# Filler work of an attention stage in smaller pieces, and an expert combination merged with the normalisation that follows it

## The chip, the cores and the metric

The program runs on one core of one Trainium2 chip and is launched once. The metric is the device time of that launch in microseconds (us). The profile is of one execution of the same program.

## The reference, cut to what matters

Two transformer blocks work on 512 tokens of width 1024, in float32. The parts that the change touches:

```python
# first block
mod = silu(c) @ ada_w + ada_b           # six rows of 1024: sh1, sc1, g1, sh2, sc2, g2
h = rms_norm(x, ln1_g) * (1.0 + sc1) + sh1
x = x + g1 * hybrid_mixer(h, w_in, w_out, ...)      # eight NSA heads, eight MoBA heads
h = rms_norm(x, ln2_g) * (1.0 + sc2) + sh2
x = x + g2 * sparse_moe(h, ...)         # per token: sum over 4 experts of gate * y[expert row]
...
# second block
h = rmsnorm(x, norm1_g)
z = h @ w_in                            # then a convolution branch, an attention branch, PEER
```

## The kernel before, in words

The tokens lie as four tiles of 128 rows on the partitions (`env.x`, named x_res in the trace). The program is a row of stages. Each stage is a block in which the five engines run their own lists of instructions and meet only by semaphores; a stage ends in a barrier of all engines (line 173), and nothing of the next stage is issued before it. There is no scheduler: the order on an engine is the order in which the code is written.

**Weights.** `Pieces` brings weights in pieces of 1 MB into four places of a ring (`load`, issued by SP, line 210). A piece for TensorE is split into two parts, so that three products give float32 accuracy: ScalarE rounds the whole piece (`round`, line 232, 128x2048) and VectorE subtracts (`split`, line 241). A piece for the modulation stays raw: `modulate` (lines 313 to 322) multiplies each of its four 512-column slices by an entry of silu(c) and adds it to a row of `mod` (line 320), four passes that depend on each other.

**The attention of the first block** (`attention`, stage att1) goes through 12 heads of 8 steps g: heads 0 to 7 are NSA heads (g = 0 to 63), heads 8 to 11 are pairs of MoBA heads. In a step ScalarE takes the exponential of the scores (line 861), TensorE transposes it (line 782) and starts the scores of step g + 2 (lines 774, 775), VectorE moves the transposed tile out of PSUM (line 889), takes the maximum of the next scores (line 883) and, in steps 1 to 4 of a head, finishes the head before it (lines 899 to 924); in step 4 it also prepares the compressed scores (lines 941 to 944), which ScalarE exponentiates (line 869). Before heads 3, 4, 7 and later more than one operand has to be transposed and moved (lines 765, 853). Two hooks put filler work of later stages between: `act_between(g)` on ScalarE behind the exponential, `dve_between(g)` on VectorE behind the maximum. Before the change VectorE runs four modulation passes in a row at g = 4, 8, 12 and 16, and a whole split at g = 34, 38, 42 and 46; ScalarE rounds a whole piece at g = 33, 37, 41 and 45.

**Experts, combination, normalisation.** `expert_blocks` writes each expert's rows to DRAM (`y_rows`). The stage `combine` (line 1709) gathers 16 tiles of 128 rows into all eight places of the ring with indirect DMAs of GpSimd (line 1723), and VectorE sums four of them per token tile with their gates, multiplies by g2 and adds to x (lines 1730 to 1734). Since the gathered rows fill the ring, the second mixer's first weight pieces can't be loaded until the stage is over. The stage `norm_split` (line 1739, named norm) then loads the gain and four pieces (SP), takes the squares of all four tiles on ScalarE (line 1763) and one square root (line 1765), scales the rows on VectorE (line 1780), transposes them on TensorE (line 1796), rounds and subtracts the transposed tiles (lines 1768, 1783), and last rounds and splits the four pieces (lines 232, 241). Then a barrier, and the stage conv begins with the product of the first piece.

Of the kernel before, what the change touches and what calls it, by code (L numbers as in the profile page):

```python
# [5 lines left out]
F32 = mybir.dt.float32  # L6
# [4 lines left out]
ALU = mybir.AluOpType  # L11
# [3 lines left out]
P = 128  # L15
# [166 lines left out]
class Pieces:  # L182
# [60 lines left out]

    def take(self, pe):
# [67 lines left out]
def modulate(env, pieces, dve, step, mod, c_act, n, first=0, halves=(0, 1)):  # L312

    own = mod[:, ada_tile(LATER[n])]
    for half in halves:
        w = pieces.take_raw(dve)
        if half:
            dve.wait_ge(pieces.summed, 2 * n + 1)
        for k in range(4):
            ins = env.nc.vector.scalar_tensor_tensor(own, w[:, k, :], c_act[:, 4 * half + k:4 * half + k + 1], own, ALU.mult, ALU.add)  # L320
            if k < 3:
                ins.then_inc(step, 1)
                dve.wait_ge(step, (2 * (n - first) + half) * 3 + k + 1)
        ins.then_inc(pieces.summed, 1)
# [624 lines left out]
def nsa_and_moba(env, z, kct, vc, gs, y_dram, pieces, mod, c_act, step):  # L949
# [759 lines left out]
def combine(env, gate, dest, y_dram, g_row):  # L1709

    nc = env.nc
    ctx, sb, ps, sem = stage(nc, "comb")
    with ctx:
        acc = sb("acc", [P, D])
        got = [sem(f"got{t}") for t in range(NT)]
        chain_s = sem("chain")
        block = ctx.enter_context(nc.Block())
        row = lambda n: env.ring[:, n // 2, (n % 2) * D:(n % 2 + 1) * D]

        @block.gpsimd  # L1720
        def _(pool):
            for n in range(NT * TOP_K):
                nc.gpsimd.indirect_dma_start(row(n), None, y_dram, bass.IndirectOffsetOnAxis(dest[:, n:n + 1], 0)).then_inc(got[n // TOP_K], 16)

        @block.vector
        def _(dve):
            chain = Chain(dve, chain_s)
            for t in range(NT):
                dve.wait_ge(got[t], 16 * TOP_K)
# [9 lines left out]
def norm_split(env, ht, h, pieces, gain, first_loads):  # L1739
# [3 lines left out]
    with ctx:  # L1743
# [16 lines left out]
        def _(act):  # L1760
# [8 lines left out]
            for i in range(RAW):  # L1769
                pieces.round(act)  # L1770
# [801 lines left out]
```

## Time and profile before

| what | value |
|---|---|
| median of 3 runs | 3841.49 us (3839.79 to 3841.69) |
| the profiled execution | 3840.8 us |
| its span, first to last instruction | 3838.6 us |
| mean granted TensorE clock | 0.934 of full |
| TensorE busy | 88% of the span |
| VectorE busy | 76% |
| ScalarE busy | 36% |

The busy shares are averages over some fifteen stages with different limits, so they say little about one of them. The clock is given as a share of 2.4 GHz: 0.50 is 1.2 GHz. The attention of the first block lies at 257 to 474 us of the span; the combination, the normalisation and the barriers around them at 1776 to 1844 us.

### The profile page before, as it was taken

How to read it: one execution, taken by the hardware profiler on the slowest of the kernel's cores; microseconds unless marked ns; L12 is line 12 of the kernel's file. 1: busy time of each engine (PE TensorE's matmuls, PEld its weight loads, DVE VectorE, ACT ScalarE, POOL GpSimd, SP SyncE). 2: the span in 40 equal slices, each digit the busy share in tenths (PEclk: the TensorE clock that was granted, in tenths of full speed). 3: DMA queues.
4: the chain of work that ended last, by engine and by line, in shares of the span. 5: the costliest groups of instructions: out<-in, count | busy, mean ns of one | idle time of the engine just before them, and what ended most of it. 6: DMA issues, size and time to landing. Idle time of an engine off the chain costs nothing. (4 is left out here: it accounts for less than half of the span.)

```text
span 3838.6 us, 39707 instructions
## 1 busy us (share of the span) xinstructions
PE 3383.1 (88%) x13912; PEld 2336.3 (61%) x13912; DVE 2909.8 (76%) x4717; ACT 1386.3 (36%) x1678; POOL 720.4 (19%) x720
## 2 busy tenths in 40 slices
PE   7979969999999999993889999878888888888876
PEld 4757757777777777772768687644344443443432
DVE  4566668999999999995788254378888888888885
ACT  2223436777777777772213343111111111111110
POOL 0000001000000000001000010034444444444442
PEclk9957989999999999996899989989999999999999
DMA  5343038999999999994323302299999999999997
GB/s 198 99 168 115 10 126 307 381 367 374 373 366 378 370 369 378 366 371 162 98 77 110 99 1 99 80 377 417 421 415 407 421 413 414 411 420 416 406 421 326
DMA packets 253621, 1106.23 MB, mean 288 GB/s; under 512 B 21233, under 2 KB 30577, under 8 KB 187601
## 3 DMA queue, kind: packets, MB, share of 16 engines
q1 hardware_dynamic: 166130, 521.50, 37.5%
q0 software_dynamic: 80640, 562.07, 35.7%
q10 hardware_dynamic: 6720, 20.97, 1.4%
q8 instruction: 75, 1.23, 0.1%
q14 instruction: 56, 0.46, 0.0%
HBM read 1071.44 MB, written 33.03 MB: 288 GB/s over the span
## 5 line engine op out<-in xcount | busy, mean ns | idle before, releaser
L2298 PE MATMUL peer_acc<-peer_rows,peer_diag 128*128 128x512 f32 x2048 | 983.7, 629 | 218.0 <-DVE peer_diag L2450 217.2
L1634 DVE TENSOR_TENSOR moe_w_lo<-ring,moe_w_hi 128x2048 fp32r<-128x2048 f32 x384 | 861.7, 2286 | 49.4 <-ACT moe_w_hi L1550 49.4
L2298 PEld LDWEIGHTS peer_acc<-peer_rows,peer_diag 128*128 128x128 f32 x2048 | 390.9, 200 | 747.1 <-issue 413.9
L2233 POOL DMA_INDIRECT peer_rows<-in_peer_uv,peer_ids x512 | 578.6, 1130 | 930.4 <-PE peer_acc L2298 682.2
L1550 ACT ACTIVATE moe_w_hi<-ring 128x2048 fp32r<-128x2048 f32 x384 | 713.8, 1913 | 106.4 <-DMA ring<-in_exp_w 68.3
L2445 DVE CUSTOM_DVE_ANT_0 peer_rows<-peer_rows,peer_h 128x1024 f32<-128x1024 f32 x512 | 618.8, 1223 | 158.4 <-DMA peer_rows<-in_peer_uv,peer_ids 149.5
L2357 ACT ACTIVATE peer_gelu<-peer_dot 128x2 f32<-128x2 f32 x256 | 52.0, 203 | 1130.6 <-DVE peer_dot L2445 1130.5
L1413 POOL COPY moe_col<-slots 128x1 uint32 (+1 forms) x32 | 53.0, 1658 | 1068.9 <-PE moe_tp L1442 973.1
L2450 DVE TENSOR_SCALAR peer_diag<-consts_sb,peer_gelu,peer_gates 128x128 f32<-128x128 f32 x512 | 161.5, 389 | 68.3 <-ACT peer_gelu L2357 67.1
L241 DVE TENSOR_TENSOR mix_lo<-ring,mix_hi 128x2048 fp32r<-128x2048 f32 (+1 forms) x56 | 125.6, 2257 | 76.1 <-ACT mix_hi L232 75.4
L1459 PE MATMUL moe_yp<-moe_w_hi,moe_hidt_hi 128*128 128x512 f32 x512 | 168.2, 409 | 2.1 <-DVE moe_hidt_lo L1629 2.1
L1459 PE MATMUL moe_yp<-moe_w_lo,moe_hidt_hi 128*128 128x512 f32 x512 | 163.0, 400 | 0.0
L1972 DVE SCALAR_TENSOR_TENSOR conv_rows<-glu,conv_taps,conv_rows 128x512 f32<-128x512 f32 x240 | 161.2, 757 | 0.5
L1459 PE MATMUL moe_yp<-moe_w_hi,moe_hidt_lo 128*128 128x512 f32 x512 | 161.4, 396 | 0.0
L2261 PEld LDWEIGHTS peer_qps<-peer_ht,ring 128*128 128x128 f32 x1024 | 125.9, 195 | 35.0 <-issue 35.0
L889 DVE COPY spare<-att_pt 128x128 f32<-128x128 f32 (+3 forms) x160 | 78.6, 491 | 87.6 <-PE att_pt L782 84.1
L232 ACT ACTIVATE mix_hi<-ring 128x2048 fp32r<-128x2048 f32 (+1 forms) x56 | 104.9, 1886 | 102.4 <-DMA ring<-in_w_in 45.4
L262 PE MATMUL conv_acc<-mix_hi,ht_hi 128*128 128x512 f32 x320 | 128.3, 401 | 11.8 <-DVE glu L1960 11.8
L774 PE MATMUL att_sc<-spare 66*128 66x128 f32 (+3 forms) x320 | 132.0, 499 | 1.5 <-ACT spare L853 1.5
L2261 PE MATMUL peer_qps<-peer_ht,ring 128*128 128x128 f32 x1024 | 126.6, 278 | 5.4 <-DMA ring<-in_peer_wq 4.7
L263 PE MATMUL conv_acc<-mix_lo,ht_hi 128*128 128x512 f32 x320 | 127.1, 397 | 0.0
L264 PE MATMUL conv_acc<-mix_hi,ht_lo 128*128 128x512 f32 x320 | 127.1, 397 | 0.0
(447 smaller groups left out, 5822.5 us busy)
## 6 DMA issues: line engine op xcount, KB each, us to landing
ring<-in_exp_w SPq DMA_DIRECT2D x384, 1024.0 KB, 7.1
ring<-in_w_in SPq DMA_DIRECT2D x38, 1024.0 KB, 5.2
ring<-in_ada_w SPq DMA_DIRECT2D x16, 1024.0 KB, 7.6
y_rows<-moe_y ACTq DMA_DIRECT2D x32, 512.0 KB, 6.9
ring<-in_ada_w SPq DMA_DIRECT2D x4, 2048.0 KB, 17.9
ring<-in_w_out SPq DMA_DIRECT2D x8, 1024.0 KB, 5.0
ring<-in_peer_wq SPq DMA_DIRECT2D x4, 2048.0 KB, 18.5
peer_rows<-in_peer_uv,peer_ids POOLq DMA_INDIRECT x512, 12.6
```

What stands on the lines that cost most here:

```text
L262: nc.tensor.matmul(out, lhs[0], rhs[0], start=start, stop=False)
L263: nc.tensor.matmul(out, lhs[0], rhs[1], start=False, stop=False)
L774: nc.tensor.matmul(sc[:, g % 2, 0:end], qt[0:AUG, q_place(i, u), t * P:end], kt[0:AUG, k_place(i, u), 0:end], start=True, stop=False)
L1459: last = nc.tensor.matmul(bank[:, q, :], lhs[l][:, k, :], w[:, slot, a * D + q * W:a * D + (q + 1) * W], start=k == 0 and l == 0 and w is ...
L1550: nc.scalar.activation(w_hi[:, slot, :], env.ring[:, slot, :], ACT.Copy).then_inc(hi_done, 1)
L1634: nc.vector.tensor_tensor(w_lo[:, slot, :], env.ring[:, slot, :], w_hi[:, slot, :].bitcast(F32), ALU.subtract).then_inc(lo_done, 1)
L1972: ins = nc.vector.scalar_tensor_tensor(conv[:, n, :], glu[:, n, tap:tap + S], taps[:, n, tap:tap + 1], conv[:, n, :], ALU.mult, ALU.add)
L2233: nc.gpsimd.indirect_dma_start(rows[:, n % SL, :], None, d["peer_uv"], bass.IndirectOffsetOnAxis(ids[:, u % 4, s:s + 1], 0)).then_inc(gath ...
L2261: last = nc.tensor.matmul(qps[:, side, :], wq[head // 2][:, k, at:at + P], ht[:, k, t * P:(t + 1) * P], start=(k == 0), stop=(k == KC - 1))
L2298: last = nc.tensor.matmul(acc[:, t % 2, q, :], diag[:, n % SL], rows[:, n % SL, D + q * W:D + (q + 1) * W], start=first, stop=final)
L2445: nc.vector.tensor_tensor_reduce(left, left, h[:, t, :], 1.0, 0.0, ALU.mult, ALU.add, dot[:, n % SL:n % SL + 1]).then_inc(dotted, 1)
L2450: nc.vector.tensor_scalar(diag[:, n % SL], ident, act_out[:, n % SL:n % SL + 1], gates[:, u % 4, n % K:n % K + 1], ALU.mult, ALU.mult).the ...
```

## The change

In the attention, the same filler work is cut finer and spread. `modulate_op` issues one modulation pass, at each even g from 6 to 36 (16 passes). `round_part` and `split_part` treat a quarter of a piece (128x512): the roundings at each even g from 44 to 74, the splits at each odd g from 55 to 85.

The stages of combination and normalisation become one, `combine_and_norm`. The gathered rows go into the room in which the second mixer later keeps its activations (`got_rows`), so the ring is free and the gain and the four pieces are issued by SP at the stage's beginning, beside GpSimd's gathers. ScalarE scales the first gathered tile of each token tile, and takes square and square root of one tile at a time; VectorE puts the scaling and subtraction of a finished tile between the passes of the next. Two of the four splits move into the stage conv.

```diff
+    def round_part(self, act, q):
+        i, parts, cols = self.of_pe[self.rounds]
+        n = parts * cols // 4
+        cut = slice(q * n, (q + 1) * n)
+        if q == 0:
+            act.wait_ge(self.landed[i % RAW], 16 * (i // RAW + 1))
+            act.wait_ge(self.used, self.rounds - RAW + 1)
+        ins = self.env.nc.scalar.activation(self.hi[:, self.rounds % RAW, cut], self.raw[:, i % RAW, cut], ACT.Copy)
+        if q == 3:
+            ins.then_inc(self.hi_done, 1)
+            self.rounds += 1
...
     def act_between(act, g):
-        if g in (33, 37, 41, 45):
-            pieces.round(act)
+        if 44 <= g < 76 and g % 2 == 0:
+            pieces.round_part(act, (g - 44) // 2 % 4)
 
     def dve_between(dve, g):
-        if g in (4, 8, 12, 16):
-            n, half = divmod(g // 4 - 1, 2)
-            modulate(env, pieces, dve, step, mod, c_act, 6 + n, 6, (half,))
-        if g in (34, 38, 42, 46):
-            pieces.split(dve)
+        if 6 <= g < 38 and g % 2 == 0:
+            at, k = divmod((g - 6) // 2, 4)
+            modulate_op(env, pieces, dve, step, mod, c_act, 6 + at // 2, at % 2, k, at)
+        if 55 <= g < 87 and g % 2:
+            pieces.split_part(dve, (g - 55) // 2 % 4)
...
-def norm_split(env, ht, h, pieces, gain, first_loads):
+def combine_and_norm(env, gate, dest, y_dram, g_row, got_rows, ht, pieces, gain, first_loads):
...
+            def scale_first(t):
+                act.wait_ge(got[t], 16 * TOP_K)
+                nc.scalar.activation(h(t), h(t), ACT.Copy, scale=gate[:, t, 0:1]).then_inc(first, 1)
+
+            act.wait_ge(eps_set, 1)
+            scale_first(0)
+            pieces.round(act)
+            scale_first(1)
+            pieces.round(act)
             for t in range(NT):
-                chain(nc.scalar.activation(junk[:], env.x[:, t, :], ACT.Square, accum_out=ms[:, t:t + 1]))
...
+                act.wait_ge(added, t + 1)
+                chain(nc.scalar.activation(h(t), env.x[:, t, :], ACT.Square, accum_out=ms[:, t:t + 1]))
+                nc.scalar.activation(rstd[:, t:t + 1], ms[:, t:t + 1], ACT.Sqrt, bias=eps[:], scale=1.0 / D).then_inc(root, 1)
+                if t + 2 < NT:
+                    scale_first(t + 2)
+                    pieces.round(act)
+                for n in range(2 * t, 2 * t + 2):
+                    act.wait_ge(turn, n + 1)
+                    nc.scalar.activation(place(ht[0], n), bank(n), ACT.Copy).then_inc(hi_ok, 1)
...
             for t in range(NT):
...
+                own = h(t)
+                dve.wait_ge(got[t], 16 * TOP_K)
+                dve.wait_ge(first, t + 1)
+                for k in range(1, TOP_K):
+                    chain(nc.vector.scalar_tensor_tensor(own, row(t * TOP_K + k), gate[:, t, k:k + 1], own, ALU.mult, ALU.add))
+                    if t == 1 and k == 1:
+                        dve.wait_ge(landed, 16)
+                        normalise(0)
+                    if t > 1 and k == 1:
+                        normalise(t - 1)
+                        rest(t - 2)
+                chain(nc.vector.tensor_tensor(own, own, g_row, ALU.mult))
+                nc.vector.tensor_tensor(env.x[:, t, :], env.x[:, t, :], own, ALU.add).then_inc(added, 1)
+            pieces.split(dve)
+            normalise(NT - 1)
+            rest(NT - 2)
+            pieces.split(dve)
+            rest(NT - 1)
...
             dve.wait_ge(landed, 32)
+            for c in range(2):
+                pieces.split(dve)
             glu_of(0)
```

VectorE, attention, the beginning of head 1 (g = 8 to 12), before. The row on `mod` with x4 is a batch of modulation passes; `att_pt` is the transposed tile, `att_nmax` the maximum:

```order
L889 COPY spare<-att_pt 128x128
L883 TENSOR_REDUCE att_nmax<-att_sc 128x1
L320 SCALAR_TENSOR_TENSOR mod<-ring,c_act,mod 128x512 x4
L889 COPY spare<-att_pt 128x128
L883 TENSOR_REDUCE att_nmax<-att_sc 128x1
L899 RECIPROCAL att_rsum<-att_rsum 128x8
L908 TENSOR_REDUCE att_csum<-att_cs 128x4
L909 TENSOR_TENSOR att_wgt<-gs,att_rsum 128x4
L910 TENSOR_TENSOR att_wgt<-gs,att_rsum 128x4
L911 RECIPROCAL att_csum<-att_csum 128x4
L912 TENSOR_TENSOR att_o<-att_o,att_wgt 128x256
```

The same place now (lines 914 and 920 are the maximum and the move, 347 the modulation):

```order
L920 COPY spare<-att_pt 128x128
L914 TENSOR_REDUCE att_nmax<-att_sc 128x1
L347 SCALAR_TENSOR_TENSOR mod<-ring,c_act,mod 128x512
L920 COPY spare<-att_pt 128x128
L914 TENSOR_REDUCE att_nmax<-att_sc 128x1
...
L943 TENSOR_TENSOR att_o<-att_o,att_wgt 128x256
L920 COPY spare<-att_pt 128x256
L914 TENSOR_REDUCE att_nmax<-att_sc 128x1
L347 SCALAR_TENSOR_TENSOR mod<-ring,c_act,mod 128x512
L945 TENSOR_TENSOR att_csum<-att_csum,consts_sb 128x4
```

One pass now stands behind the maximum of every second step, also of step 2 (shown) and of step 4 of the head.

ScalarE, the beginning of the merged stage now (`mix_hi<-ring` is the rounding of a weight piece, line 1782 the scaling of a gathered tile, line 1791 the squares):

```order
L1782 ACTIVATE got_rows<-got_rows,gate 128x1024
L232 ACTIVATE mix_hi<-ring 128x2048
L1782 ACTIVATE got_rows<-got_rows,gate 128x1024
L232 ACTIVATE mix_hi<-ring 128x2048
L1791 ACTIVATE got_rows,norm_ms<-x_res 128x1024
L1792 ACT_TABLE_LOAD
L1792 ACTIVATE norm_rstd<-norm_ms,norm_eps 128x1
L1782 ACTIVATE got_rows<-got_rows,gate 128x1024
L232 ACTIVATE mix_hi<-ring 128x2048
L1798 ACTIVATE ht_hi<-norm_turned 128x4x128 x2
```

The first two roundings, which before came last in the stage norm, now stand ahead of the first square and square root.

## Rows read from the trace of the kernel before

**Rows 1.** Stretches, heads 0 to 9: us; busy of PE, PEld, DVE, ACT, POOL; clock; DMA.
```profile
256.75:280.17 23.42, 22.12 (x83) 16.64 (x82) 10.48 (x22) 6.11 (x19) 0.53 (x2) 0.50 0.33 117
280.17:302.65 22.48, 20.19 (x110) 16.02 (x109) 16.57 (x39) 6.21 (x20) 0.53 (x2) 0.73 0.28 94
302.65:323.32 20.67, 19.89 (x110) 16.42 (x109) 13.73 (x35) 6.21 (x21) 0.53 (x2) 0.75 0.61 230
323.32:340.51 17.19, 16.48 (x121) 13.96 (x120) 11.21 (x32) 7.06 (x22) 1.79 (x6) 0.96 0.59 243
340.51:362.23 21.72, 19.41 (x108) 15.52 (x106) 15.55 (x33) 9.59 (x22) 0.54 (x2) 0.77 0.00 2
362.23:385.73 23.50, 21.19 (x110) 17.16 (x109) 15.61 (x33) 9.59 (x22) 0.54 (x2) 0.72 0.00 1
385.73:402.17 16.44, 15.62 (x113) 12.85 (x112) 11.14 (x32) 6.09 (x20) 0.54 (x2) 0.98 0.00 0
402.17:418.34 16.17, 15.89 (x123) 13.43 (x121) 11.16 (x32) 7.66 (x24) 2.33 (x8) 1.00 0.01 1
418.34:432.20 13.86, 13.86 (x106) 11.56 (x104) 10.31 (x28) 6.85 (x22) 2.53 (x8) 1.00 0.01 2
432.20:445.42 13.22, 13.22 (x102) 11.04 (x101) 8.45 (x19) 6.88 (x21) 2.11 (x8) 1.00 0.01 2
```
**Rows 2.** Timeline of VectorE in the attention: a filler batch, idle places of head 6.
```profile
292.88 3.10 DVE L320 SCALAR_TENSOR_TENSOR mod<-ring,c_act,mod 128x512 f32<-128x512 f32 x4
...
390.21 0.29 DVE L889 COPY spare<-att_pt 128x128 f32<-128x128 f32 x1 [1.76 <-PE att_pt L782]
...
402.12 0.69 DVE L889 COPY spare<-att_pt 128x512 f32<-128x512 f32 x1 [0.94 <-PE att_pt L782]
```
**Rows 3.** Two stretches of head 2, columns as in the first group.
```profile
312.00:314.00 2.00, 1.67 (x12) 1.47 (x13) 1.82 (x5) 0.88 (x4) 0.00 (x0) 1.00 0.94 294
314.00:316.00 2.00, 2.00 (x11) 1.62 (x10) 1.82 (x5) 0.00 (x0) 0.00 (x0) 0.64 1.01 401
```
**Rows 4.** Timeline of the combination: the first gather, VectorE's first and last tile.
```profile
1775.92 0.94 POOL L1723 DMA_INDIRECT ring<-y_rows,dest  x1 [118.97 <-PEq L1713]
...
1785.91 0.75 DVE L1730 TENSOR_SCALAR comb_acc<-ring,gate 128x1024 f32<-128x1024 f32 x1 [33.87 <-DMA ring<-y_rows,dest]
1786.70 3.93 DVE L1732 SCALAR_TENSOR_TENSOR comb_acc<-ring,gate,comb_acc 128x1024 f32<-128x1024 f32 x3
...
1813.72 1.22 DVE L1734 TENSOR_TENSOR x_res<-x_res,comb_acc 128x1024 f32<-128x1024 f32 x1
```
**Rows 5.** Timeline of the normalisation and the barriers around it, ScalarE and VectorE.
```profile
1816.32 1.06 ACT L1763 ACTIVATE norm_junk<-x_res 128x1024 f32<-128x1024 f32 x1 [49.95 <-PEq L173]
...
1821.02 1.28 ACT L1765 ACT_TABLE_LOAD   x1
1822.32 0.30 ACT L1765 ACTIVATE norm_rstd<-norm_ms,norm_eps 128x4 f32<-128x4 f32 x1
...
1822.64 0.18 DVE L1777 RECIPROCAL norm_rstd<-norm_rstd 128x4 f32<-128x4 f32 x1 [6.22 <-ACT norm_rstd L1765]
1822.86 4.87 DVE L1780 SCALAR_TENSOR_TENSOR h<-x_res,norm_rstd,norm_gain_row 128x1024 f32<-128x1024 f32 x4
1827.65 5.23 DVE L1783 TENSOR_TENSOR ht_lo<-norm_turned,ht_hi 128x512 fp32r<-128x512 f32 x8
1833.76 8.90 DVE L241 TENSOR_TENSOR mix_lo<-ring,mix_hi 128x2048 fp32r<-128x2048 f32 x4 [0.89 <-ACT mix_hi L232]
1843.96 0.06 DVE L1976 MEMSET conv_eps<- 128x1 f32 x1 [1.30 <-PEq L173]
1862.89 0.69 DVE L1960 TENSOR_TENSOR glu<-conv_val,conv_held 128x512 f32<-128x512 f32 x1 [13.07 <-ACT conv_held L1919]
```
**Rows 6.** Stretches of the gathers alone and of the loads of gain and pieces alone.
```profile
1776.00:1802.00 26.00, 0.00 (x0) 0.00 (x0) 15.63 (x14) 0.00 (x0) 16.81 (x16) 0.50 0.86 323
1816.30:1832.00 15.70, 6.39 (x32) 5.78 (x32) 9.21 (x13) 10.81 (x19) 0.00 (x0) 0.56 0.95 300
```
**Rows 7.** The page's group of the roundings (busy, mean ns; idle before).
```profile
L232 ACT ACTIVATE mix_hi<-ring 128x2048 fp32r<-128x2048 f32 (+1 forms) x56 | 104.9, 1886 | 102.4 <-DMA ring<-in_w_in 45.4
```
**Rows 8.** A 512 KB gather of the expert stage: quickest, median, slowest from issue to landing.
```profile
DMA to landing us min/median/max: 4.3/8.0/9.0
```

More of the change, by code:

```diff
@@ L309, in ada_tile, with modulate_op, modulate @@
     return slice(j * W, (j + 1) * W)
-def modulate(env, pieces, dve, step, mod, c_act, n, first=0, halves=(0, 1)):
+def modulate_op(env, pieces, dve, step, mod, c_act, n, half, k, at):
     own = mod[:, ada_tile(LATER[n])]
-    for half in halves:
-        w = pieces.take_raw(dve)
+    if k == 0:
+        pieces.now = pieces.take_raw(dve)
         if half:
             dve.wait_ge(pieces.summed, 2 * n + 1)
-        for k in range(4):
[L320 to L324, printed above, removed]
+    else:
+        dve.wait_ge(step, 3 * at + k)
+    ins = env.nc.vector.scalar_tensor_tensor(own, pieces.now[:, k, :], c_act[:, 4 * half + k:4 * half + k + 1], own, ALU.mult, ALU.add)
+    ins.then_inc(step if k < 3 else pieces.summed, 1)
+def modulate(env, pieces, dve, step, mod, c_act, n, first=0):
+    for half in range(2):
+        for k in range(4):
+            modulate_op(env, pieces, dve, step, mod, c_act, n, half, k, 2 * (n - first) + half)
 def first_norm(env, mod, c_act, ht, z, pieces):
@@ L1706, in _ @@
             dve.sem_inc(tick, 1)
[L1709 to L1729, printed above, removed]
-                chain(nc.vector.tensor_scalar(acc[:], row(t * TOP_K), gate[:, t, 0:1], None, ALU.mult))
-                for k in range(1, TOP_K):
-                    chain(nc.vector.scalar_tensor_tensor(acc[:], row(t * TOP_K + k), gate[:, t, k:k + 1], acc[:], ALU.mult, ALU.add))
-                chain(nc.vector.tensor_tensor(acc[:], acc[:], g_row, ALU.mult))
-                chain(nc.vector.tensor_tensor(env.x[:, t, :], env.x[:, t, :], acc[:], ALU.add))
 C2_GATE, C2_Q, C2_F, C2_GA, C2_GB = D, 2 * D, 5 * D, 5 * D + FOX_HEADS, 6 * D + FOX_HEADS
 PAD = CONV_W - 1
-def norm_split(env, ht, h, pieces, gain, first_loads):
+def combine_and_norm(env, gate, dest, y_dram, g_row, got_rows, ht, pieces, gain, first_loads):
     nc = env.nc
@@ L1743, in norm_split @@
     with ctx:
-        gain_row = sb("gain_row", [P, D]); junk = sb("junk", [P, D])
+        gain_row = sb("gain_row", [P, D])
         ms = sb("ms", [P, NT]); rstd = sb("rstd", [P, NT]); eps = sb("eps", [P, 1])
         turned = ps("turned", [P, 4, W])
-        landed, eps_set, root, ready, turn, hi_ok, lo_ok, act_s, chain_s = (sem(n) for n in (
-            "landed", "eps_set", "root", "ready", "turn", "hi_ok", "lo_ok", "act_chain", "chain"))
+        landed, first, added, root, eps_set, ready, turn, hi_ok, lo_ok, act_s, chain_s = (sem(n) for n in (
+            "landed", "first", "added", "root", "eps_set", "ready", "turn", "hi_ok", "lo_ok", "act_chain", "chain"))
+        got = [sem(f"got{t}") for t in range(NT)]
         block = ctx.enter_context(nc.Block())
+        row = lambda n: got_rows[:, n, :]
+        h = lambda t: got_rows[:, t * TOP_K, :]
         place = lambda a, n: a[:, 4 * (n % 2):4 * (n % 2) + 4, n // 2 * P:(n // 2 + 1) * P]
@@ L1757, in _ @@
             sp.wait_ge(landed, 16)
+        @block.gpsimd
+        def _(pool):
+            for n in range(NT * TOP_K):
+                nc.gpsimd.indirect_dma_start(row(n), None, y_dram, bass.IndirectOffsetOnAxis(dest[:, n:n + 1], 0)).then_inc(got[n // TOP_K], 16)
         @block.scalar
```

47 lines of the change are left out of this document (25 added, 22 removed).

## Prediction

> **What bounds the kernel now.** The page first: TensorE is busy for 88% of the span, VectorE for 76%. That is an average, and the change works in two places only, so I read stretches. In the attention one stretch per head shows what a head costs and at which clock [rows 1]. Heads 6 to 9 hold no filler work: 16.44, 16.17, 13.86 and 13.22 us, the clock full. Heads 0, 1, 2, 4 and 5 hold filler batches: 23.42, 22.48, 20.67, 21.72 and 23.50 us, the clock between 0.50 and 0.77. So a batch costs twice: its own time, and a clock that has fallen. VectorE is busy for only 11 of 16.4 us in a clean head, but its idle time lies in few places; the timeline shows 1.76 us ahead of step 1's move and 0.94 us ahead of step 7's [rows 2], and between, in steps 1 to 4, it finishes the head before without a pause. Work put there delays ScalarE's exponential and TensorE one for one.
>
> The second place is a serial chain. From the first gather at 1775.92 to the first instruction of the stage conv at 1843.96 pass 68.0 us [rows 4, 5]: 10.0 until the first four gathers have landed, 29.0 in which VectorE adds without a pause, 1.4 of barrier, 6.2 of squares and root on ScalarE alone, 20.0 of VectorE's scaling, subtraction and four splits, 1.3 of barrier. TensorE is almost idle in it, so each us saved is a us of the program.
>
> **The attention, step by step.** A modulation pass takes 3.10 / 4 = 0.78 us [rows 2], a split 8.90 / 4 = 2.23, so a quarter 0.56 [rows 5], a rounding 1.89, so a quarter 0.47 [rows 7]. Busy time is unchanged, and what counts is where the pieces fall.
> - Head 0: the batch at g = 4 goes (3.1 on the path), one pass at g = 6 lies beside TensorE's work: 23.4 - 3.1 = 20.3.
> - Heads 1 and 2: passes in steps 0 and 6 lie in VectorE's idle places, those in steps 2 and 4 don't: 16.4 + 2 x 0.78 = 18.0 each. Head 3 has none now (17.19, its clock 0.96) and gets four: 18.8.
> - Head 4: three passes, two exposed: 18.0. Head 5: two quarter roundings, which lie beside VectorE's work: 16.6. Head 6: four roundings and one split quarter: 16.8.
> - Head 7: split quarters in steps 1 and 3 are exposed (1.1), a little of a rounding too: 17.6. Head 8 the same: 15.1. Heads 9 and 10 (10 like 9): TensorE is busy for all of 13.22 us and VectorE for 8.45, so of the quarters only 0.2 us each show: 14.0 and 13.7.
> Heads 0 to 3 take 83.8 now and would take 75.1; heads 4 to 10 take 118.1 and would take 111.8. Sum: 15.0 us saved, **if the clock stays full** after head 0.
>
> It does not always stay. Head 2 holds one batch, in step 0: 16.4 + 3.1 - 1.76 (the idle place) = 17.8 expected, 20.67 measured, so its fall of clock costs 2.9. It fell at 314.6, when TensorE had been busy for 1.67 of 2 us at full clock [rows 3], with VectorE at 1.82 of 2. Passes in steps 2 and 4 stretch just this part of a head, by 1.6 us, about what head 2 lost there; head 3 got through it, with more transposes to do. So I expect such a fall in two of heads 1 to 4, 5.8 us: **9.2 us saved**. Bounds: no fall, 15.0; a fall in each of heads 1 to 4 and 7, 15.0 - 14.5 = 0.5. The Trainium skill ("TensorE: Matmul & The Clock Gate", HAM oscillation) ties a lost clock to a long gap in TensorE's work. By that rule head 2 should have kept its clock, and the sum would be the 15.0; the row speaks against it, since no such gap stands in the 2 us ahead of the fall.
>
> **The merged stage.** VectorE's own row first. Tile 0: three passes, gain, addition, 3.93 + 2 x 1.26 = 6.45. Tile 1: the same, reciprocal and scaling (1.44), and a wait: addition done, square 1.25, table load 1.28, root 0.30, against one pass of 1.31 that covers it, so 1.5; 9.4. Tiles 2 and 3: 6.45 + 1.44 + two subtractions (5.23 / 8 each, 1.31) + 0.3 of wait, 9.5 each. Tail: two splits 4.46, scaling 1.44, four subtractions 2.6: 8.5. Together 43.4. The scaling of the first tile on ScalarE comes before (1.1), one barrier behind (1.4); one barrier goes. If the gathers landed as now, conv would begin at 1785.9 + 1.1 + 43.4 + 1.4 = 1831.8, **12.1 us earlier**. The two splits moved into conv (4.5) are covered by the 13.07 us in which VectorE waits for the first gate there [rows 5].
>
> But now two streams meet. The gathers alone keep the DMA engines busy for 0.86 x 26.0 = 22.4 us, gain and pieces alone for 0.95 x 15.7 = 14.9 [rows 6]. Together that is 37.3 us from 1776: the last byte lands at 1813 at the earliest, where the last gather now lands by 1802. And ScalarE takes its work in order: the first rounding stands ahead of the second tile's scaling, the second ahead of the first square, on which tile 1's scaling on VectorE waits. With equal shares the first group of four gathers lands at 1790.7, the second at 1802; VectorE ends tile 0 at 1798.3; ScalarE scales, rounds, takes square and root until 1807.7; VectorE then has 1.44 + 5.1 + 9.5 + 9.5 + 8.5 = 34 left, and with the barrier conv begins at 1843.2: 0.8 saved. With 70% for the pieces the first group lands at 1796, the second at 1801.5, the root comes at 1807: 1.5 saved. With pieces served only behind the gathers (1801), the second piece lands at 1809, the root comes at 1814 and conv begins at 1850: 6.5 lost. A price of such contention stands in the expert stage: a gather of 512 KB lands in 4.3 us at best and in 8.0 in the median, beside weight loads [rows 8]. A gather there pays more than an equal share, so the middle cases are nearest: **2 us saved**, bounds -6.5 and 12.1. The Trainium skill ("DMA: Bandwidth & Descriptors", Queues, rings and completion order) says that an engine takes turns between queues, a packet of several descriptors each. By it neither stream starves, and the sum would be that of the middle cases.
>
> **Sum.** 9.2 + 2 = 11.2 us saved of the profiled execution's 3840.8 us: 3829.6. The median shown, 3841.49, is 0.7 above that execution, so 3830 for a median. Behind both places the stages follow by barriers and keep their lengths. The fill of y_rows and the last weight loads start some 35 us later, and the stage's end at 474 still covers them. A measurement here can tell about 0.2%, 7.7 us, from no change.
>
> **Rivals.**
> - *The clock holds* in heads 1 to 8 (the skill's rule gives the same): 15.0 + 2 saved, 3824. For it: heads 3, 6, 7 and 8 hold it with VectorE as full in steps 1 to 4. Against it: head 2. Chance 0.20.
> - *The streams do not hurt each other*: 9.2 + 12.1 saved, 3819.5. It needs the first group by 1787 and two pieces by 1797. Against it: both streams alone run the engines at 0.86 and more [rows 6]. Chance 0.08.
> - *The gain goes*: falls in five heads leave 0.5, and the merge gives nothing: 3840. Chance 0.12.
> - *Slower: the clock falls and does not come back.* Single passes in every second step keep TensorE short of work in heads 1 to 8. A head at half clock costs head 0's 20.3 against 16.4, so 3.9 more; eight of them cost 31 against 17 saved, 3855. It decides from 4.4 such heads on, and shows as slower from 6.3. For it: head 0 stayed at 0.50 from end to end with TensorE nominally busy. Against it: heads 1 and 2 came back to full clock within a head. Chance 0.10.
> The forecast has the other 0.50, with a range of its own of 3824 to 3837. About three quarters of it lie over 7.7 us below. Faster by over 0.2%: 0.37 + 0.20 + 0.08 = 0.65; slower 0.11, the slow case and a little of the starved pieces; within 0.2%: 0.24. The range for eight in ten reaches over the good rivals and up to the third: 3818 to 3841.
>
> **What the profile of the changed kernel would show.** Right: head 0 near 20, heads 5 and 6 near 16.7 at full clock, two of heads 1 to 4 near 21 with a clock of 0.75; gathers that land later than 1786 in their first group, ScalarE waiting for a piece ahead of line 1782 or 1791, conv beginning at 1840 to 1844 less what the attention saved. Wrong: heads 1 to 4 all at 18 (the clock holds), or heads 6 to 8 near 20 (it is lost); the root of tile 0 by 1799 (no collision), or after 1812 (pieces starved); a conv stage longer than before.

## The result, and the profile after

The changed kernel takes 3819.55 us (median of 9 runs, 3810.76 to 3831.39), the kernel before, measured beside it, 3839.79. The ratio is 0.9937, its 95% interval 0.992 to 0.9954: 24 us or 0.6% faster, between 18 and 31 us. Forecast were 11 us. The two parts of the forecast came near what was measured for them; a third of the gain or more came from a stage to which the forecast gave no term. Five executions of the run e2 and two of e6 took some 80 us longer, and one of the kernel before 565 us longer; they are left out of the ratios and stand in the medians.

The profiled execution of the changed kernel took 3814.12 us. From its page, the span and the busy time of each engine (us, share of the span, instructions); TensorE's share is the 88% of before:

```profile
span 3812.3 us, 39707 instructions
...
PE 3361.5 (88%) x13912; PEld 2319.9 (61%) x13912; DVE 2906.1 (76%) x4728; ACT 1391.8 (37%) x1697; POOL 711.0 (19%) x720
```

The first attention of the changed kernel, a stretch per head from 0 to 9, columns as in [rows 1]:

```profile
260.69:275.22 14.53, 14.04 (x86) 10.91 (x85) 8.19 (x20) 6.12 (x19) 0.53 (x2) 0.83 0.32 116
275.22:294.73 19.51, 18.74 (x108) 15.36 (x106) 13.77 (x35) 6.10 (x21) 0.55 (x2) 0.78 0.16 55
294.73:315.33 20.60, 19.83 (x110) 16.39 (x109) 13.85 (x35) 6.10 (x21) 0.54 (x2) 0.75 0.15 52
315.33:333.50 18.17, 16.69 (x121) 13.91 (x120) 13.78 (x36) 7.16 (x22) 2.13 (x6) 0.96 0.18 59
333.50:353.24 19.74, 18.97 (x108) 15.46 (x106) 13.13 (x34) 6.10 (x20) 0.55 (x2) 0.77 0.30 89
353.24:369.91 16.67, 15.85 (x113) 13.07 (x112) 11.14 (x32) 7.02 (x22) 0.54 (x2) 0.97 1.02 421
369.91:385.98 16.07, 14.85 (x111) 12.26 (x109) 11.11 (x32) 7.97 (x24) 0.55 (x2) 1.00 0.03 12
385.98:403.00 17.02, 16.11 (x123) 13.39 (x121) 13.35 (x36) 9.65 (x28) 3.05 (x8) 1.00 0.00 1
403.00:417.89 14.89, 14.77 (x109) 12.01 (x107) 12.27 (x32) 9.06 (x26) 2.30 (x8) 1.00 0.01 2
417.89:431.14 13.25, 13.18 (x100) 10.73 (x100) 10.59 (x23) 7.91 (x23) 2.42 (x8) 1.00 0.00 1
```

Heads 4 and 5 gave up their whole roundings and splits: 45.2 became 36.4 us. Heads 1, 2 and 4 still lose the clock (0.75 to 0.78). In head 0 the mean clock was 0.83 instead of 0.50. Of eight other profiles with the same work in head 0 one repeats this (e1, 14.6 us) and seven don't (22.1).

The merged stage. ScalarE's timeline (start, us, engine, line, operation, tile; in brackets the idle time before and what ended it), then VectorE's and the issue of the four pieces by SP, to be read beside [rows 4, 5]:

```profile
1775.94 1.15 ACT L1782 ACTIVATE got_rows<-got_rows,gate 128x1024 f32<-128x1024 f32 x1 [22.31 <-DMA got_rows<-y_rows,dest]
...
1782.69 1.15 ACT L1782 ACTIVATE got_rows<-got_rows,gate 128x1024 f32<-128x1024 f32 x1 [3.80 <-DMA got_rows<-y_rows,dest]
1785.43 1.91 ACT L232 ACTIVATE mix_hi<-ring 128x2048 fp32r<-128x2048 f32 x1 [1.60 <-DMA ring<-in_w_in]
1787.25 1.04 ACT L1791 ACTIVATE got_rows<-x_res 128x1024 f32<-128x1024 f32 x1
...
1796.75 1.91 ACT L232 ACTIVATE mix_hi<-ring 128x2048 fp32r<-128x2048 f32 x1 [5.73 <-DMA ring<-in_w_in]
...
1800.70 0.29 ACT L1792 ACTIVATE norm_rstd<-norm_ms,norm_eps 128x1 f32<-128x1 f32 x1
```

```profile
1790.12 0.16 DVE L1806 RECIPROCAL norm_rstd<-norm_rstd 128x1 f32<-128x1 f32 x1 [4.90 <-ACT norm_rstd L1792]
...
1801.10 0.16 DVE L1806 RECIPROCAL norm_rstd<-norm_rstd 128x1 f32<-128x1 f32 x1 [3.27 <-ACT norm_rstd L1792]
...
1810.42 0.17 DVE L1806 RECIPROCAL norm_rstd<-norm_rstd 128x1 f32<-128x1 f32 x1 [0.41 <-ACT norm_rstd L1792]
...
1827.62 0.06 DVE L2024 MEMSET conv_eps<- 128x1 f32 x1 [1.29 <-PEq L173]
...
1847.13 0.69 DVE L2008 TENSOR_TENSOR glu<-conv_val,conv_held 128x512 f32<-128x512 f32 x1 [9.50 <-ACT conv_held L1967]
```

```profile
1762.87 19.19 SPq L210 DMA_DIRECT2D ring<-in_w_in  x4
```

The first gather is issued at 1763.19. VectorE now waits for roots: 4.90 us for tile 0, 3.27 for tile 1. Ahead of each root, ScalarE stood before a piece that had not landed (1.60 and 5.73). From the first gather to conv pass 64.4 us, where it was 68.0.

What the plan did not hold is in a stage whose code is unchanged. The second block has an attention too (the same function, without filler work), directly behind conv. Its first two heads before, columns as above:

```profile
2203.41:2224.13 20.72, 20.48 (x76) 15.01 (x75) 6.98 (x15) 6.87 (x20) 2.11 (x8) 0.50 0.00 1
2224.13:2243.71 19.58, 19.58 (x107) 16.28 (x107) 8.45 (x19) 6.87 (x20) 2.11 (x8) 0.69 0.00 0
```

The same two in the changed kernel:

```profile
2189.13:2202.68 13.55, 13.32 (x81) 10.34 (x80) 6.98 (x15) 6.88 (x21) 2.11 (x8) 0.82 0.01 1
2202.68:2215.89 13.21, 13.21 (x102) 11.03 (x101) 8.45 (x19) 6.87 (x20) 2.11 (x8) 1.00 0.00 0
```

The account of the profiled executions in us; the third column is another execution of the changed kernel (the run e4_after_again):

| part | before | changed | changed, again |
|---|---|---|---|
| start of the first attention | 256.8 | 260.7 | 257.5 |
| heads 0 to 10 | 201.9 | 183.7 | 192.3 |
| from there to the first gather | 1317.3 | 1318.8 | 1318.6 |
| first gather to conv | 68.0 | 64.4 | 64.3 |
| conv | 359.5 | 361.5 | 362.0 |
| second attention, first two heads | 40.3 | 26.8 | 26.7 |
| the rest | 1594.9 | 1596.4 | 1596.3 |
| span | 3838.6 | 3812.3 | 3817.8 |

So of the 20.8 us between the first and the last column, 9.6 lie in the heads, 3.7 in the merge and 13.6 in the start of the second attention; that is 26.9, of which 6.1 are given back in small amounts over the other parts. Single executions of one kernel differ there too: conv took 359.5 us in this profile of the kernel before and 360.9 in another (e3).

### The profile page after: what moved, and what is told of

Its sections match the earlier page's. It is cut to its first block and busy times, and to the rows that moved or that the text cites. A ratio compares the mean times of both kernels' runs of the same rounds, so it can differ in the third digit from the quotient of the medians.

```text
span 3812.3 us, 39707 instructions
## 1 busy us (share of the span) xinstructions
PE 3361.5 (88%) x13912; PEld 2319.9 (61%) x13912; DVE 2906.1 (76%) x4728; ACT 1391.8 (37%) x1697; POOL 711.0 (19%) x720
## 5 line engine op out<-in xcount | busy, mean ns | idle before, releaser
L2284 POOL DMA_INDIRECT peer_rows<-in_peer_uv,peer_ids x512 | 567.8, 1109 | 942.4 <-PE peer_acc L2349 693.7
L241 DVE TENSOR_TENSOR mix_lo<-ring,mix_hi 128x2048 fp32r<-128x2048 f32 (+1 forms) x52 | 116.7, 2255 | 75.6 <-ACT mix_hi L232 75.0
L805 PE MATMUL att_sc<-spare 66*128 66x128 f32 (+3 forms) x320 | 120.5, 460 | 1.5 <-ACT spare L884 1.5
```

The costliest lines, as they stand in the source:

```text
L2284: nc.gpsimd.indirect_dma_start(rows[:, n % SL, :], None, d["peer_uv"], bass.IndirectOffsetOnAxis(ids[:, u % 4, s:s + 1], 0)).then_inc(gath ...
```

## Is the whole gain the change's own?

**One half each, and each kernel once more.** e1 takes the attention's part alone, with the two stages as before. e2 takes the merged stage alone, its attention as before. Its edit against the changed kernel, cut to the roundings (passes and splits go back in the same way):

```diff
-        if 44 <= g < 76 and g % 2 == 0:
-            pieces.round_part(act, (g - 44) // 2 % 4)
+        if g in (33, 37, 41, 45):
+            pieces.round(act)
...
```

e3 is the kernel before and e4 the changed kernel, each profiled once more.

> The attention's filler work cut and spread as in the change, combination and normalisation as before. Theory A (the attention carries most of the gain, about 16 us; the merge gives 3 to 4): 3822 to 3826 median, heads 0 to 10 of the first attention together 184 to 190 us against 202 before, conv 68 us behind the first gather. Rival B (both parts share the gain about equally, and a good part of what the changed kernel's profile shows in the second attention, 12 us, belongs to the merge): 3830 to 3834. Rival C (nearly all is the clock's chance in single executions): within 5 us of the kernel before, and a wide spread.

> The merged stage as in the change, the attention's filler work in whole batches as before. Theory A: 3 to 4 us below the kernel before, 3836 median; from the first gather to conv 64 us against 68. Rival B: 8 to 16 us below, with the second attention shorter than in the kernel before in most executions. Rival C: no difference.

> The kernel before, profiled once more. If the state of TensorE's clock in head 0 of the first attention and in heads 0 and 1 of the second differs between executions of the same program, this profile shows it in at least one of the places: head 0 either near 23.4 us at 0.50 or near 17.6 us with a higher clock, the second attention's first two heads 41 us or 27 us. If the clock is the same in every execution of one program (then the change decides it), all three come out as in the first profile.

> The changed kernel, profiled once more. By chance of the clock: another pattern in head 0 of the first attention (14.5 us in its first profile) or in heads 0 and 1 of the second (27 us). By a clock that the program decides: the same pattern, with heads 1, 2 and 4 again near 20 us.

Measured, medians: e1 3832.67, ratio 0.9968 (0.9946 to 0.999); e2 3849.84 over all its executions, 3835.59 and ratio 0.9978 (0.9951 to 1.0005) without the five at 3920 to 3934; the kernel before 3841.59 beside them. Single times: e3 3826.68, e4 3819.6. By rows, the heads' sum is 192.1 us in e1 against 201.7 in e2, and from the first gather to conv pass 64.1 us in e2 against 67.4 in e1: 9.5 and 3.3 us, together less than the whole. The times can't tell this: by the ratios the parts give 12 and 8 us, e2's interval reaches over 1, and their sum is about the whole.

Theory A had e1 at 3822 to 3826 with heads of 184 to 190 us, and missed both; e1 lies where rival B had it, but B's reason, a second attention that the merge shortens, is not in e2's profile (40.3 us for its first two heads). That e1's heads come out at the 192 us of other profiles is a coincidence. Head 0 came up early there (14.6 us for 22.1), and head 5 lost about as much, for which e4 took 16.7 us:

```profile
349.40:374.14 24.74, 24.74 (x110) 19.73 (x109) 11.20 (x31) 7.12 (x22) 0.53 (x2) 0.57 0.70 286
```

e3 is the surprise: the unchanged kernel before, in a profile with a span of 3824.5. Its heads (201.7) and its stages up to conv are those of [rows 1, 4, 5] within 1 us; the second attention's first two heads are not:

```profile
2203.88:2217.42 13.54, 13.31 (x81) 10.33 (x80) 6.97 (x15) 6.87 (x21) 2.11 (x8) 0.82 0.01 1
2217.42:2230.63 13.21, 13.21 (x102) 11.03 (x101) 8.44 (x19) 6.86 (x20) 2.11 (x8) 1.00 0.00 0
```

So the same program has a half-clock start of this stage (40 us for two heads) in some executions and a clean one (27 us) in others. e1's profile has the first kind, e4's the second.

The two kinds differ in when the clock comes back, and hardly in when it falls. For the kernel before, its preparation of the second attention, ahead of the first exponential, and 2 us about the return of the clock:

```profile
2193.60:2203.41 9.81, 4.46 (x23) 2.88 (x22) 0.89 (x3) 4.25 (x7) 3.98 (x16) 0.76 0.29 108
2235.00:2237.00 2.00, 2.00 (x12) 1.70 (x11) 1.10 (x3) 0.51 (x2) 0.48 (x2) 0.68 0.00 0
```

The same in e3:

```profile
2193.20:2203.88 10.68, 5.41 (x22) 3.29 (x22) 0.89 (x3) 4.21 (x7) 3.98 (x16) 0.59 0.29 99
2207.88:2209.88 2.00, 2.00 (x12) 1.64 (x11) 0.76 (x2) 1.04 (x3) 0.53 (x2) 0.78 0.00 0
```

TensorE is busy for half of the preparation, and the clock falls in it in both (mean 0.76 and 0.59). It is back about 5 us behind the first exponential in e3 and about 33 us behind it in the kernel before, with TensorE busy for nearly all of the time between.

## What each part of the attention gives, and the order on ScalarE

e5 is the changed kernel with its roundings of weight pieces in the merged stage behind the square and root:

```diff
             scale_first(0)
-            pieces.round(act)
             scale_first(1)
-            pieces.round(act)
...
                 if t + 2 < NT:
                     scale_first(t + 2)
-                    pieces.round(act)
                 for n in range(2 * t, 2 * t + 2):
...
+                pieces.round(act)
```

e6 has the merge and the single passes, with whole roundings and splits as before; e7 has the merge and the quarters, with the batches of four passes as before. e8 is the changed kernel with short extra work for TensorE at the start of both attentions: transposes of a constant into the score bank, whose results nothing reads:

```diff
+            for _ in range(2):
+                for i in range(4):
+                    nc.tensor.transpose(sc[:, 0, i * P:(i + 1) * P], env.const("iota"), ident)
             for m in range(len(heads[0].operands)):
                 operand(0, m)
+                for i in range(4):
+                    nc.tensor.transpose(sc[:, 0, i * P:(i + 1) * P], env.const("iota"), ident)
```

> The changed kernel with ScalarE's order in the merged stage turned: both first scalings, then square and root of each tile, and each rounding only behind the copies of its tile. Theory (ScalarE's order is what the collision of gathers and pieces works through: the root of tile 0 waited for the second piece's rounding, that of tile 1 for the third piece, which landed 5.7 us late): the root of tile 0 comes 3 us earlier, that of tile 1 another 3, and conv begins 57 to 59 us behind the first gather, against 64.4 in the changed kernel. Rival (the gathers themselves are late, and the order only hides it): VectorE waits for the second or third group of gathers instead, 62 to 64 us.

> The changed kernel with only the modulation passes spread; roundings and splits whole, at g = 33 to 46 as before. Theory (heads add up by the places of their filler work): heads 0 to 3 as in the changed kernel (14.5 or 22, 19.5 to 20.6, 20.6, 18.2), head 4 with passes and a whole rounding and split 23, head 5 at 23.5, heads 6 to 10 at 16.4, 16.2, 13.9, 13.2, 13.2. Rival (the clock's state decides more than the work): heads 1 to 4 spread by more than 3 us from these.

> The changed kernel with only roundings and splits in quarters; the modulation in whole batches at g = 4 to 16. Theory: heads 0 to 2 as in the kernel before (23.4, 22.5, 20.7), head 3 17.1, head 4 without any filler 16.4 if the clock holds, head 5 16.7, heads 6 to 10 as in the changed kernel (16.1, 17.0, 14.9, 13.2, 13.2). The sum of heads 0 to 10 193 against 201.8 before and 183.7 or 192.3 in the changed kernel. Rival (a fallen clock in head 1 or 2 is carried on): head 3 or 4 over 19.

> The changed kernel with transposes of a constant table added on TensorE at the beginning of both attention stages (8 ahead, 4 behind each operand of the first head; into the score bank, which the first scores overwrite). Theory (what differs between executions is when the clock rises at the start of an attention: head 0 of the first 14.5 or 22, heads 0 and 1 of the second 27 or 40): head 0 at 14 to 15, the second attention's first two heads 27 in the profile, the executions less spread than 3810 to 3831, median 3806 to 3812. Rival (the clock's start does not hang on TensorE's work there): the same two patterns and the same spread, median 3817 to 3821.

Measured: e5 3814.97 (3802.66 to 3821.74), ratio 0.993 (0.9905 to 0.9955); e6 3838.35 over all its executions (3838.0 without the two long ones), ratio 0.9992 (0.9973 to 1.0011); e7 3819.28, ratio 0.9941 (0.9925 to 0.9956); e8 3804.56, ratio 0.9901 (0.9881 to 0.9922).

**The merge.** In e5 the first gather is at 1768.7 and conv begins at 1826.9: 58.2 us instead of 64.4. VectorE's timeline there, the same two waits for a root:

```profile
1792.17 0.17 DVE L1804 RECIPROCAL norm_rstd<-norm_rstd 128x1 f32<-128x1 f32 x1 [1.39 <-ACT norm_rstd L1790]
...
1800.40 0.17 DVE L1804 RECIPROCAL norm_rstd<-norm_rstd 128x1 f32<-128x1 f32 x1 [0.51 <-ACT norm_rstd L1790]
```

They fell from 4.90 and 3.27 to 1.39 and 0.51, 6.3 us together, and the stage by 6.2. The forecast without any collision was 55.9 us (1831.8 less 1775.9), so what the collision still costs here is about 2 us, an estimate from those two. It costs more in the changed kernel because the roundings stand ahead of the square in ScalarE's order. In time the 6 us are not resolved: the intervals of e5 and of the changed kernel overlap, so this rests on the rows.

**The attention.** e6's heads 4 and 5, with whole roundings and splits:

```profile
338.57:362.35 23.78, 20.81 (x108) 16.79 (x106) 17.54 (x36) 9.59 (x22) 0.54 (x2) 0.72 0.25 76
362.35:385.95 23.60, 21.29 (x110) 17.26 (x109) 15.61 (x33) 9.59 (x23) 0.54 (x2) 0.72 0.74 303
```

The same heads of e7, without passes and with the quarters put into heads 5 to 10:

```profile
343.04:358.91 15.87, 15.05 (x111) 12.33 (x109) 11.09 (x32) 6.09 (x20) 0.54 (x2) 1.00 0.00 1
358.91:374.78 15.87, 15.05 (x111) 12.34 (x109) 11.09 (x32) 7.03 (x22) 0.54 (x2) 1.00 0.01 2
```

The sum of heads 0 to 10 is 201.8 in e6, just that of before: single passes alone give nothing. Head 0 is 22.1 instead of 23.4, heads 1 and 2 20.6 each, with the clock at 0.75, and what they save is lost in heads 3 and 4. In e7 the sum is 192.2, though head 1 fell to half clock (29.5 us for 22.5) where head 0 had come up early (19.2 for 23.4). The quarters carry the gain, and the times say the same: e7's median is the changed kernel's, e6's is near the kernel before.

e6's profiled execution is also one of those that take 80 us longer. The third head of its second attention:

```profile
2247.63:2273.23 25.60, 25.60 (x102) 20.33 (x102) 8.45 (x19) 6.87 (x20) 2.11 (x8) 0.50 0.00 1
```

25.60 us instead of 13.21, TensorE busy for all of it, and the granted clock 0.50. The heads from the second on took 25.60 each. The clock fell where it falls in the other profiles without e8's transposes, in the preparation of the stage (9 us ahead of the first exponential at 2201.31), and here it did not come back in the whole stage, with TensorE busy throughout from the second head on.

**e8** began both attentions at full clock (head 0 12.66 us, the second attention's first head 11.51):

```profile
257.32:269.98 12.66, 11.89 (x84) 9.41 (x85) 7.98 (x20) 6.00 (x19) 0.53 (x2) 1.00 0.38 140
269.98:289.09 19.11, 18.34 (x108) 14.97 (x106) 13.68 (x35) 6.09 (x20) 0.54 (x2) 0.79 0.18 56
289.09:316.78 27.69, 27.69 (x110) 22.36 (x109) 13.77 (x35) 6.09 (x20) 0.53 (x2) 0.50 0.11 38
```

In its profiled execution heads 2 to 4 then lost the clock (27.7, 20.2 and 22.6 us), which took back the 9 us won in head 0 (sum of heads 192.5). It is the slowest of the six, 8 us over their median, which suggests that most executions keep the 9 us. The median of 3804.56 is a little below the 3806 to 3812 expected.

## The change with both starts made sure

e9 is the kernel before with e8's transposes in both attentions, e10 with those of the second alone. e9 against e8 is the change without the luck of the starts. e11 is the changed kernel with each filler piece in a place where VectorE waits anyway; e12 has everything that helped: e8's starts, e11's places, e5's order.

```diff
+    passes = [g for g in range(6, 47) if g % 8 in (0, 6, 7)][:16]
...
-        if 6 <= g < 38 and g % 2 == 0:
-            at, k = divmod((g - 6) // 2, 4)
+        if g in passes:
+            at, k = divmod(passes.index(g), 4)
```

The roundings move to g = 56 to 86 and the splits to g = 65 to 95.

> The kernel before with the constant transposes at the beginning of both attention stages, nothing else. Theory (the change is worth 12 to 14 us, which its profiles show in the first attention and the merged stage; the rest of the measured 24 us is that its executions more often begin the second attention at full clock): with the start made sure in both kernels the second attention's first head takes 11.5 us here too, this kernel lands at 3815 to 3822, and the warm changed kernel's 3804.6 is 11 to 16 us below it, not 24. Rival (all 24 us belong to the change's own work): 3826 to 3830.

> The kernel before with the constant transposes at the beginning of the second attention alone. Theory: a slow start there costs 13 to 14 us and most executions of the kernel before have it, so 3824 to 3828 median and much less spread; the second attention's first two heads 25 us. Rival (the start of the second attention is no cause of the difference): 3838 to 3842.

> The changed kernel with the same filler pieces elsewhere: modulation passes only in steps 0, 6 and 7 of heads 0 to 5, split quarters only at odd g from 65 to 95 (heads 8 to 11), roundings at even g from 56 to 86. Theory (a piece in steps 1 to 4 of an NSA head is exposed and lets the clock fall; in a step where VectorE waits it is free): heads 1 to 6 near 16.5 us at full clock, 17.3 for head 3, head 7 16.2, head 8 14.5, the rest 13.2; the sum of heads 0 to 10 168 to 178 against 192 for the changed kernel with a slow head 0, median 3800 to 3807. Rival (any filler work on VectorE costs its time in these heads): the sum stays over 185.

> Constant transposes at both starts, filler pieces in the idle places, and the merged stage with square and root ahead of the roundings. If the three add up: head 0 12.7, sum of heads 0 to 10 167 to 172, conv 58 us behind the first gather, second attention's first head 11.5; median 3774 to 3784. If not (the time given back in a later stage, or the clock falls elsewhere): over 3790.

Measured: e9 3818.03, ratio 0.9944 (0.9921 to 0.9967); e10 3829.03, ratio 0.9963 (0.9944 to 0.9983); e11 3806.67, ratio 0.9908 (0.9876 to 0.994); e12 3791.8 (3780.32 to 3804.09), ratio 0.9867 (0.9832 to 0.9901).

A start of the second attention at full clock is worth 12 us to the kernel before by the medians and 14 by the ratios (e10, just over the 3824 to 3828 expected). One of the first attention is worth another 11 by the medians, but 7 by the ratios and by the rows of e9, whose head 0 takes 17.2 us for 23.4. With both, the change takes the time from 3818.03 to 3804.56: **13.5 us by the medians**, 16.5 by the ratios. The rows of the kernels without transposes say 13.3 (9.6 + 3.7). All three are near the 11.2 of the forecast.

The agreement is looser than it looks. The intervals of the two ratios still overlap at their ends, so the difference is uncertain by several us. The 13.3 is a sum over executions with head 0 at half clock, and the profiles of e9 and e8 don't confirm it: their heads take 195.2 and 192.5 us, since e8's is the one that lost the clock in heads 2 to 4.

e11's median met its expectation (3800 to 3807), but its heads tell that the places alone don't keep the clock. Its profiled execution is the slowest of seven, with a span of 3839.0 and heads of 210.5 us where 168 to 178 were expected; heads 1, 2 and 5:

```profile
283.06:310.75 27.69, 27.69 (x110) 22.36 (x109) 13.17 (x34) 6.10 (x21) 0.53 (x2) 0.50 0.01 1
310.75:332.27 21.52, 20.81 (x113) 17.22 (x112) 13.05 (x35) 6.09 (x20) 0.53 (x2) 0.71 0.13 49
...
368.51:396.19 27.68, 27.68 (x110) 22.35 (x109) 13.19 (x34) 6.09 (x20) 0.53 (x2) 0.50 0.02 3
```

With a clean start in front, in e12, the same heads 1, 2 and 5 with the same work:

```profile
273.17:289.03 15.86, 15.04 (x111) 12.33 (x109) 12.96 (x35) 6.08 (x20) 0.55 (x2) 1.00 0.00 1
289.03:304.90 15.87, 15.05 (x111) 12.34 (x109) 12.97 (x35) 6.09 (x21) 0.55 (x2) 1.00 0.20 68
...
336.92:352.79 15.87, 15.05 (x111) 12.34 (x109) 12.97 (x35) 6.09 (x20) 0.54 (x2) 1.00 0.01 2
```

15.87 with a whole pass in steps 0, 6 and 7, the same as e7's heads with none: in the idle places the passes are free while the clock is full, as [rows 2] suggested. All eleven heads of e12 take 166.2 us, and from the first gather to conv pass 58.1. Yet its median missed the 3774 to 3784 expected if the three add up, by 8 us. In its profile (span 3788.1) 3 us of that are given back between the heads and the first gather (1321.7 for 1318.6). Its times spread over 24 us, so some executions may still lose the clock somewhere; that was not seen. It is the best version here, 28 us or 0.7% below the changed kernel by the medians.

## Does the moment decide how the second attention starts?

The changed kernel began this stage clean in both of its profiles; e1 and e2 did not. Of 93 single times of the kernel before, taken beside the experiments, 11 lie under 3830, near e3's 3826.68. Two reasons are possible: the moment at which the stage begins, now some 9 to 15 us earlier, or the code that runs ahead of it. e13, e14 and e15 put 4, 7 and 11 idle multiplications at the end of the merged stage:

```diff
             rest(NT - 1)
+            for _ in range(4):
+                chain(nc.vector.tensor_tensor(row(1), row(2), g_row, ALU.mult))
```

> The changed kernel with four idle multiplications (128x1024, about 1.25 us each) at the end of the merged stage, so that conv and everything behind it begin 5 us later; nothing else moves. The second attention would begin near 2200, where the kernel with the merge alone began it (2199.4). Theory (whether the first two heads there run at half clock hangs on the moment at which the stage begins): half-clock starts in more than half of the executions, median 3819.5 + 5 + 13 = 3837 to 3839, some at 3920. Rival (it hangs on the code that runs, not on the moment): clean starts as in the changed kernel, median 3824 to 3826.

> The same with seven, 8.8 us: the second attention would begin near 2203.5, where the kernel before begins it. Theory of the moment: half-clock starts in about five of six executions, as before, median 3819.5 + 8.8 + 13 = 3840 to 3842. Rival of the code: median 3828 to 3830.

> The same with eleven, 13.8 us: begin near 2208.5, a moment that no kernel here has tried without help for the clock. Theory of the moment: gives no number ahead, 3833 if the starts are clean and 3846 if not; what counts is whether the three delays differ by more than their own 5.0, 8.8 and 13.8. Rival of the code: 3833, in line with the other two.

| | delay by rows | median | ratio | over the changed kernel |
|---|---|---|---|---|
| changed | 0 | 3819.55 | 0.9937 (0.992 to 0.9954) | 0 |
| e13 | 4.9 | 3831.66 | 0.9984 (0.9966 to 1.0003) | 12.1 |
| e14 | 8.8 | 3842.64 | 1.001 (0.9995 to 1.0025) | 23.1 |
| e15 | 13.8 | 3834.43 | 0.9986 (0.9967 to 1.0004) | 14.9 |

A sum of delays would be 3824.5, 3828.4 and 3833.4. e13 is 7 us over it, e14 14 and e15 only 1. The rival of the code had e14 at 3828 to 3830, so it fell: a delay of 8.8 us undoes the whole change. The theory of the moment was right in e14 (3840 to 3842 expected) and half right in e13, which it put at 3837 to 3839. That e14 is slower than e15, which waits 5 us longer, is not resolved: their intervals overlap.

How the second attention starts in the longer executions was not seen. All three profiled ones had clean starts (first heads of 13.7, 13.6 and 13.5 us) and lie at the low end of their times (the lowest, the lowest and the second lowest). That the longer ones start at half clock is argued from the size of the steps; a loss in the first attention would look the same.

And the moment, counted from the first instruction, can't be all. The stage's first exponential came at 2199.39 in e2, with a half-clock start, and at 2199.32 in e14, with a clean one; at 2195.20 in e1, half clock, and at 2194.73 in e4, clean; at 2203.41 in the kernel before, half clock, and at 2203.88 in e3, clean. Of the thirteen profiles without transposes in this stage, four started at half clock (the kernel before, e1, e2, e6) and nine clean, eight of them in kernels with both the quarters and the merge. What decides is open.

## Why the prediction was right in its mechanism and short in its size

- **The attention, forecast 9.2 us, measured 9.6** (201.9 to 192.3; five profiles of the changed attention with a half-clock start in head 0 lie between 192.0 and 193.2). That the sum is so near is in part luck, since errors in its parts cancel. Head 0: 20.3 forecast, 22.1 measured. The forecast took the batch's 3.1 us to be all on the path, but [rows 1] has TensorE busy for 22.12 of the 23.42 us, at half clock, so no more than 1.3 could be won; in e4 it is busy for 21.88 of 22.11. Falls: two of heads 1 to 4 were expected for 5.8; heads 1, 2 and 4 came out at 20.6, 20.6 and 19.7 instead of 18.0, which is 6.9. Quarters: heads 5 and 6 at 16.7 and 16.1 for 16.6 and 16.8, heads 7 to 10 at 58.3 for 60.4; e6 takes 56.5 for them without the quarters, so these cost half of what was forecast.
- **The clock.** The forecast said that passes in steps 2 and 4 bring falls without a long pause of TensorE. In the changed kernel's head 1 the clock fell in the second of these two stretches (columns as in [rows 3]):

```profile
283.00:285.00 2.00, 1.26 (x11) 1.26 (x12) 1.81 (x5) 0.30 (x1) 0.00 (x0) 1.00 0.00 0
285.00:287.00 2.00, 2.00 (x11) 1.43 (x10) 1.82 (x4) 0.37 (x2) 0.00 (x0) 0.75 0.00 0
```

 TensorE had been idle for 0.74 us of the first, with VectorE busy for 1.81, and busy for all of the second. The rival that the clock holds fell with it, and so did the slower one: heads 5 to 10 were at 0.97 to 1.00 in both profiles. That a fall needs such passes is not shown: in e1 the clock fell in head 5, which holds none, with TensorE busy for 24.74 of 24.74 us.
- **The merge, forecast 2 us, measured 3.6.** Measured from the first gather: the first group landed after 12.7 us (14.8 forecast with equal shares, 10.0 before), the root of tile 0 was there after 26.8 (31.8), conv began after 64.4 (67.3). The gathers got more than an equal share, and the pieces less; the issue of four pieces took SP 19.19 us beside the gathers and 7.27 before. What followed the root took 37.6 us instead of 35.5, because the third piece delayed the root of tile 1 too, a wait the forecast did not have. That the collision acts through ScalarE's order is shown by e5.
- **The step that failed** is the one sentence behind the sum: "Behind both places the stages follow by barriers and keep their lengths." They did within 3 us each, except for the second attention, whose first two heads went from 40.3 to 26.8 us. The working gave this term 0; it is 13.6 us in the profiles, and by the medians what is left of the 20 to 24 us beyond the change's own 13.5, which is 7 to 11. It is no fixed gain of the change: the unchanged kernel has it in e3, and how often each kernel has it was not seen. It was within reach: [rows 1] showed head 0 at 0.50 with TensorE busy, the second attention's first heads stood in the same trace at 0.50 and 0.69, and a term should have asked what becomes of them when the stage moves.
- The range (3818 to 3841) held the time. The rival nearest to it, streams that do not hurt each other (3819.5), gives the right number for the wrong reason: the merge saved 3.6 us, not 12.1.

## What to carry to other kernels

A single profile shows one draw of every stage whose clock depends on how it starts: look at stages that the change does not touch, take a second profile of the same kernel, and give such a stage its own term and bounds. Put filler work where its engine waits already, in quarters if they fit there: the quarters saved 9.6 us, and single passes in every second step, also where VectorE never waits, saved nothing. Before a piece of work is counted as on the path, look whether the engine beside it is idle at all: a head in which TensorE is busy for 22.1 of 23.4 us has no 3.1 us to give. Where two streams are brought together, take the work that waits for the later one out of the way of the work that all others need; that order was worth 6.2 us of the stage, more than the merge itself.

## What the runs showed of the hardware

- A stage can begin at half clock and stay there with TensorE busy: 40.3 us or 26.8 for two heads of one program in two executions (the kernel before and e3), and 25.60 us per head where 13.21 is usual in e6's profile. The clock had fallen 5 to 9 us ahead of the first exponential in all thirteen profiles without transposes in this stage, while TensorE was busy for about half of the time; it came back 5 us behind it, 33 us behind it, or not in the stage. The Trainium skill ("TensorE: Matmul & The Clock Gate", What's actually happening) says that the number of slow matmuls at a start varies from run to run of one kernel; the rows agree. It adds that a model should not be fitted to such a count, since a slow start costs under 1% of a typical kernel. The 13.6 us here are 0.35% and agree, but they were a third to a half of what the change seemed to give.
- Eight short transposes ahead of the first operand and four behind each gave a full clock at the first exponential in every profile that had them: 12.7 us for head 0 against 22.1 (e8, e12; e9's head 0, with its batch of four passes, took 17.2 against 23.4 at a clock of 0.90), and 11.5 for the second attention's first head against 13.5 or 20.7 (e8, e9, e10, e12). It did not keep the clock up later: e8's head 2 was at 0.50.
- Idle delays of 4.9, 8.8 and 13.8 us ahead of conv cost 12.1, 23.1 and 14.9 us in the medians. That the start of the second attention makes the difference was not seen, nor what decides it.
- Four pieces of 1 MB took SP 7.27 us to issue without other loads beside them and 19.19 beside sixteen indirect gathers of 512 KB (18.77 in e5).
